# Memory attention: dividing the probabilities before their transposes, and leaving the values product transposed

## Chip, cores, metric
One core of a Trainium2 chip. The metric is the device time of one execution in microseconds (us), the median of three runs. The core has a matrix engine (TensorE, "PE" in the profile; its weight loads are "PEld"), a vector engine (VectorE, "DVE"), an activation engine (ScalarE, "ACT"), a general engine (GpSimd, "POOL") and a queue engine for transfers (SyncE, "SP"). Each works through its own queue in order, and they wait for each other by semaphores.

## The reference, cut to what matters
The kernel is one layer: a state-space mixer beside block attention, then attention over a memory of 256 rows, then a gated convolutional feed-forward network. The change lies in the attention over the memory alone:

```python
def memory_cross_attention(h, mem_n, w_q, w_kv, w_o, qn, kn):
    bsz, t = h.shape[0], h.shape[1]
    m = mem_n.shape[1]
    q = rms_norm((h @ w_q).reshape(bsz, t, X_HEADS, X_HEAD_DIM), qn)
    kv = mem_n @ w_kv
    k = rms_norm(kv[..., :D_X].reshape(bsz, m, X_HEADS, X_HEAD_DIM), kn)
    v = kv[..., D_X:].reshape(bsz, m, X_HEADS, X_HEAD_DIM)
    s = jnp.einsum('bqhd,bmhd->bhqm', q, k).astype(jnp.float32) * (X_HEAD_DIM ** -0.5)
    prob = jax.nn.softmax(s, axis=-1).astype(v.dtype)
    o = jnp.einsum('bhqm,bmhd->bqhd', prob, v).reshape(bsz, t, D_X)
    return o @ w_o
```

There are 512 tokens, 4 heads of width 128, 256 memory rows, and everything is fp32.

## The kernel before
The order of every engine's queue is written out by hand. The 512 tokens are four tiles of 128. The attention over the memory runs in 16 steps, `s = 4 * tile + head`. In step `s` TensorE makes the scores of step `s + 2` (`x_scores`, 128x256 into PSUM), then a "piece" of six 128x512 products with weights (`xq_piece`: the q projection of tiles 2 and 3, up to step 6; `xo_piece`: the output projection, from step 7 on), then the two transposes of the probabilities of step `s` (`prob_transposes`), then the values product of step `s - 1` (`x_values`). In steps 1, 5 and 9 it first transposes the normalised q of the next tile (`qx_transposes`), and in steps 5, 9 and 13 it transposes at the end the attention's output of tile 0, 1 and 2 (`xo_transposes`); that of tile 3 comes among the output pieces after the loop. Products with weights are made of three fp32r products, of high and low halves.

Around it, for every step: VectorE takes the row maximum (`row_max`, line 1855), ScalarE scales it and makes the exponential with its row sum (`x_probabilities`, line 1022) into `pbuf`, which has two slots; the transposed probabilities are copied out of PSUM by ScalarE for even and by VectorE for odd steps (`xp_evac`, line 412 on VectorE). VectorE also evacuates the transposed q (`transposed`, line 1423), and, four steps at a time, divides the output rows by the row sums (`normalise`, lines 1686 and 1420). The transposed output is split into a high half by ScalarE (`xo_hi`) and a low half by VectorE (`xo_lo`, line 1426); both are the left operand of the output projection. The output weights are split into halves too: the high half by ScalarE (`split_hi`, line 498, in steps 5 to 8), the low half by GpSimd (`output_low`, line 976). VectorE adds each finished output tile to the residual (`w_residual`, line 1426).

PSUM has eight banks. `use(bank, name)` in `plan` gives each result its bank in the order of filling; a product that fills a bank waits until the result before it in that bank has been read:

```python
        def fill(pe, name, r=0):

            bank, n = uses[name]
            if n > 0:
                pe.wait_ge(bank_free[bank], r + n)
            return pb[bank]
```

Results are named `xs` (scores), `xp` (transposed probabilities), `xpv` (values product of a tile), `xo` (its transposes), `qxt` (transposed q) and `w00` to `w31` (tile and column half of the output projection). After the 16 steps come the rest of the output projection, the transposes of its normalised rows (`x3_transposes`), and the up projection of the feed-forward network, which is over half of the kernel.

Of the kernel before, what the change touches and what calls it, by code (L numbers as in the profile page):

```python
# [20 lines left out]
TT = T // 128  # L21
# [6 lines left out]
M = 256  # L28
MT = M // 128
XH, XD = 4, 128  # L30
# [75 lines left out]
def layer(nc, A, out):  # L106
# [11 lines left out]
    with ctx:  # L118
# [151 lines left out]
        yasq_ready, yasum_ready = sem("yasq_ready"), sem("yasum_ready")  # L270
        qr_ready = sem("qr_ready")
        conv_ready, gate_ready = sem("conv_ready"), sem("gate_ready")
# [3 lines left out]

        QXT_BANK, XO_BANK, W_BANK = (0, 1, 2, 0), (1, 0, 1, 7), (2, 1, 2, 0, 2, 1, 3, 2)

# [7 lines left out]
        def plan():  # L286
# [38 lines left out]
            for t in range(TT):  # L325
                use(t % 3, f"qx{t}"); use(QXT_BANK[t], f"qxt{t}")

            for s in range(TT * XH):
                use(3 + s % 3, f"xs{s}"); use(6, f"xp{s}")
            for t in range(TT):  # L330
                use(7, f"xpv{t}"); use(XO_BANK[t], f"xo{t}")
                for half in range(2):
                    use(W_BANK[2 * t + half], f"w{t}{half}")
# [679 lines left out]
        def _(act):  # L1013
# [302 lines left out]
            def xo_hi(t):  # L1316
                tile_hi(f"xo{t}", bs[:, 0, :].rearrange("p (a n) -> p a n", a=4)[:, :, t * 128:(t + 1) * 128])

# [17 lines left out]
            for s in range(TT * XH):  # L1336
                if s % 2 == 1:
                    xp_evac(act, lambda o, i: A_(o, i, ACT.Copy), s - 1)
                if s + 1 < TT * XH:
                    x_probabilities(s + 1)  # L1340
                if s in (3, 7):
                    qx_rows(2 + s // 4)
                if s in (6, 10, 14):
                    xo_hi((s - 6) // 4)
                if s in XO_AT:
                    split_hi(act, U_XO + XO_AT.index(s))
                if s == 13:
                    h_square("x3", "w", "x30", 0, 0)
# [60 lines left out]
        def _(dve):  # L1409
# [272 lines left out]

            def normalise(bank, l0, heads, width, t):

                p = read(dve, bank)
                link(V.reciprocal(rl[:, 0:heads], lsum[:, l0:l0 + heads]))
                drained(tt(yrow[:, t, :].rearrange("p (h n) -> p h n", h=heads),
                           p[:, :].rearrange("p (h n) -> p h n", h=heads),
                           rl[:, 0:heads].unsqueeze(2).to_broadcast([128, heads, width]), ALU.mult), bank)
                after_drain(dve, bank)  # L1690

            def tile_lo(name, hi, lo, last=True):
# [133 lines left out]
            def xo_lo(t):  # L1826
                v = [bs[:, i, :].rearrange("p (a n) -> p a n", a=4)[:, :, t * 128:(t + 1) * 128] for i in range(2)]
                tile_lo(f"xo{t}", v[0], v[1])

# [22 lines left out]
            def row_max(s):  # L1852
# [3 lines left out]
                    .then_inc(logit_ready, 1)  # L1856

            row_max(0)
            for s in range(TT * XH):
                if s + 1 < TT * XH:  # L1860
                    row_max(s + 1)
                if s in (5, 9, 13):
                    t = (s - 5) // 4
                    normalise(f"xpv{t}", 32 + XH * t, XH, XD, t)
                if s >= 2 and s % 2 == 0:
# [5 lines left out]
                if s in (2, 6, 10):  # L1871
                    root(f"qx{1 + s // 4}", qr_ready)
                if s in (6, 10, 14):
                    xo_lo((s - 6) // 4)
                if s in (10, 12):
                    w_residual(0, [s // 2 - 5])
                if s == 14:
                    w_residual(1, [0])
                    x3_mean(0)
            xp_evac(dve, V.tensor_copy, TT * XH - 1)  # L1880
            normalise(f"xpv{TT - 1}", 32 + XH * (TT - 1), XH, XD, TT - 1)
            x3_rows(0)
            w_residual(1, [1])
            xo_lo(TT - 1)
            w_residual(2, [0])
# [112 lines left out]
        def _(pe):  # L1998
# [277 lines left out]
            def prob_transposes(pre, sc, s, tiles, ring, last_of_fill=True):  # L2276
                after_drain(pe, f"{sc}{s}")
                p = fill(pe, f"{pre}{s}")
# [29 lines left out]
            def x_values(s):  # L2308
# [3 lines left out]
                for a in range(MT):  # L2312
                    last = mm(p[:, h * XD:(h + 1) * XD], ptb[:, s % 2, a * 128:(a + 1) * 128],
                              xv[:, a, h * XD:(h + 1) * XD], a == 0, a == MT - 1)
                if h == XH - 1:
# [152 lines left out]

            def xo_transposes(t):
                after_drain(pe, f"xpv{t}")  # L2470
                tile_transposes(f"xo{t}", yrow[:, t, :])

            def x3_transposes(t):
# [12 lines left out]
            for s in range(TT * XH):  # L2486
# [8 lines left out]
                else:  # L2495
                    if (s + 1) % XH == 0:
                        after_drain(pe, f"xo{(s + 1) // XH - 2}")
                    xo_piece((s + 1) // XH - 2, (s + 1) % XH)
                prob_transposes("xp", "xs", s, MT, 2)
                if s >= 1:  # L2500
                    x_values(s - 1)
                if s in (5, 9, 13):
                    xo_transposes((s - 5) // 4)
            x_values(TT * XH - 1)
            for i in range(1, 4):
                xo_piece(2, i)
                if i == 2:
                    xo_transposes(3)
            x3_transposes(0)
            after_drain(pe, "xo3")  # L2510
            for i in range(4):
# [84 lines left out]
```

## Time and profile before
| | |
|---|---|
| median of 3 runs | 676.1 us (676.05 to 676.61) |
| profiled execution, its own time | 676.84 us |
| its span in the trace | 675.0 us |
| TensorE busy | 664.4 us (98%) |
| VectorE busy | 489.7 us (73%) |
| ScalarE busy | 345.0 us (51%) |
| GpSimd busy | 178.6 us (26%) |
| granted TensorE clock | full speed, mean 1.00 |
| share of TensorE in the chain that ended last | 82% |

The time of an execution is its span and a little around it. Busy time counts an engine's own work; idle time of an engine that is not the bound costs nothing. In a timeline each row is a start, a length (of all its instructions, where it ends in x2 or more), the engine, the kernel's line, the operation, what it writes and reads, and, where the engine stood idle before it, how long and for whom. Names of tiles are the program's: `pb` is a PSUM bank, `F` a region of a large scratch buffer (q, k, v, rows and transposed probabilities all lie there), `bs` holds the attention's output in halves, `wring` the weights in halves.

### The profile page before, as it was taken

To read this page: it belongs to the slowest core of one execution; us is meant where nothing else is said; L and a number is where in the kernel's file an instruction comes from. 1 tells how busy PE (TensorE), PEld (TensorE's weight loads), DVE (VectorE), ACT (ScalarE), POOL (GpSimd) and SP (SyncE) were. 2 spreads that over 40 slices of the span, in tenths; PEclk is the share of its full clock that TensorE was granted. 3 is DMA by queue.
4 is the path that set the end of the run, shared out by engine and by line. 5 is a ranking of instruction groups with operands and counts; after the bars stand their busy time and mean duration, and the time that the engine had idled before them with its cause. 6 is when DMAs were issued, how large, how long until landed. Compare 5 with 4: busy or idle time off the path is not lost.

```text
span 675.0 us, 10889 instructions
## 1 busy us (share of the span) xinstructions
PE 664.4 (98%) x4039; PEld 550.3 (82%) x4039; DVE 489.7 (73%) x807; ACT 345.0 (51%) x602; POOL 178.6 (26%) x184
## 2 busy tenths in 40 slices
PE   7999999999999999999999999999999999999997
PEld 6978877877778788888998888888888888888886
DVE  3999998849765657556877675666566687867967
ACT  4747654676844544664454433333333454554662
POOL 4899997033221101240101111011101121100000
PEclk9999999999999999999999999999999999999999
DMA  8737563577210215030337557555556446654563
GB/s 257 225 82 183 118 186 102 156 223 258 64 63 2 98 59 187 1 124 1 126 125 249 191 186 242 191 183 187 190 191 227 146 183 210 226 186 141 178 197 124
DMA packets 73919, 105.76 MB, mean 157 GB/s; under 512 B 21929, under 2 KB 48852, under 8 KB 72340
## 3 DMA queue, kind: packets, MB, share of 16 engines
q1 hardware_dynamic: 70612, 98.89, 45.3%
q10 hardware_dynamic: 3264, 6.31, 2.9%
q8 instruction: 25, 0.41, 0.2%
q14 instruction: 18, 0.15, 0.1%
HBM read 88.27 MB, written 17.31 MB: 156 GB/s over the span
## 4 chain that ended last, share of the span: by engine, by line
PE 82%; DMA 4%; POOL 4%; ACT 4%; SPq 3%; DVE 2%; issue 1%; DVEq 0%; ACTq 0%; POOLq 0%
PE pb L519 24%; PE pb L521 24%; PE pb L520 23%; PE pb L2000 7%; PE pb L2003 4%; POOL F L802 2%; ACT F L1022 2%; SPq L679 2%; DMA raw<-in_w_in 1%; DMA F<-F 1%; DMA raw<-in_x_wkv 1%; DVE F L1420 1%; DMA F<-scr_y 1%; SPq L692 0%; ACT xs L1022 0%
## 5 line engine op out<-in xcount | busy, mean ns | idle before, releaser
L519 PE MATMUL pb<-xs,wring 128*128 128x512 f32 (+1 forms) x448 | 165.3, 369 | 0.1
L521 PE MATMUL pb<-xs,wring 128*128 128x512 f32 (+1 forms) x448 | 164.2, 366 | 0.0
L520 PE MATMUL pb<-xs,wring 128*128 128x512 f32 (+1 forms) x448 | 164.1, 366 | 0.0
L1426 DVE SCALAR_TENSOR_TENSOR F<-pb,ccol,F 128x511 f32<-128x511 f32 x88 | 65.9, 749 | 71.7 <-ACT F L1022 69.9
L509 DVE TENSOR_TENSOR wring<-raw,wring 128x1024 fp32r<-128x1024 f32 x73 | 97.5, 1338 | 6.1 <-ACT wring L498 5.9
L519 PE MATMUL pb<-wring,xs 128*128 128x512 f32 x240 | 99.1, 413 | 0.5 <-DVE wring L512 0.3
L519 PEld LDWEIGHTS pb<-xs,wring 128*128 128x128 f32 x448 | 84.5, 189 | 14.5 <-issue 0.6
L521 PEld LDWEIGHTS pb<-xs,wring 128*128 128x128 f32 x448 | 84.5, 189 | 13.7
L520 PEld LDWEIGHTS pb<-xs,wring 128*128 128x128 f32 x448 | 84.5, 189 | 13.5
L521 PE MATMUL pb<-wring,xs 128*128 128x512 f32 x240 | 94.0, 392 | 0.0
L520 PE MATMUL pb<-wring,xs 128*128 128x512 f32 x240 | 93.7, 390 | 0.0
L1022 ACT ACTIVATE F<-pb,ccol 128x512 f32<-128x512 f32 x44 | 34.3, 779 | 115.3 <-PE pb L521 115.1
L498 ACT ACTIVATE wring<-raw 128x1024 fp32r<-128x1024 f32 x78 | 81.8, 1054 | 15.1 <-DMA raw<-in_w_in 6.5
L519 PE MATMUL pb<-wring,bs 128*128 128x512 f32 x170 | 68.6, 404 | 0.6 <-DVE wring L1420 0.5
L828 POOL TENSOR_TENSOR F<-F 128x256 f32<-128x256 f32 x27 | 21.8, 809 | 172.8 <-DVE F L1420 171.4
L521 PE MATMUL pb<-wring,bs 128*128 128x512 f32 x170 | 66.3, 390 | 0.0
L520 PE MATMUL pb<-wring,bs 128*128 128x512 f32 x170 | 66.2, 390 | 0.0
L1022 ACT ACTIVATE F<-pb 16x128 f32<-16x128 f32 (+5 forms) x84 | 31.1, 383 | 56.9 <-PE pb L2003 49.0
L2000 PE MATMUL pb<-F 128*64 128x64 f32 (+6 forms) x1056 | 58.5, 256 | 1.5 <-DVE F L1420 0.7
L2000 PEld LDWEIGHTS pb<-F 128*64 128x64 f32 (+4 forms) x1056 | 45.2, 143 | 14.0 <-issue 10.6
L519 PEld LDWEIGHTS pb<-wring,xs 128*128 128x128 f32 x240 | 45.1, 188 | 12.0 <-issue 1.6
L521 PEld LDWEIGHTS pb<-wring,xs 128*128 128x128 f32 x240 | 45.1, 188 | 10.0
(160 smaller groups left out, 989.6 us busy)
## 6 DMA issues: line engine op xcount, KB each, us to landing
raw<-in_ffn_w_up SPq DMA_DIRECT2D x22, 1024.0 KB, 5.2
F<-in_ffn_w_down SPq DMA_DIRECT2D x11, 1024.0 KB, 5.0
scr_w<-F SPq DMA_DIRECT2D x11, 1024.0 KB, 3.9
F<-in_x SPq DMA_DIRECT2D x8, 512.0 KB, 5.9
raw<-in_w_in ACTq DMA_DIRECT2D x4, 1024.0 KB, 6.0
raw<-in_w_out SPq DMA_DIRECT2D x4, 1024.0 KB, 4.9
raw<-scr_w SPq DMA_DIRECT2D x8, 512.0 KB, 3.8
raw<-scr_w SPq DMA_DIRECT2D x15, 256.0 KB, 4.7
```

The source lines that it names most:

```text
L498: ins = nc.scalar.activation(w_unit(u, 0), raw_unit(u), ACT.Copy)
L509: ins = nc.vector.tensor_tensor(w_unit(u, 1), raw_unit(u), w_unit(u, 0).bitcast(f32), ALU.subtract)
L519: nc.tensor.matmul(ps, lh, rh, start=first, stop=False)
L520: nc.tensor.matmul(ps, lh, rl_, start=False, stop=False)
L521: return nc.tensor.matmul(ps, ll, rh, start=False, stop=last)
L679: sync.dma_start(toep[d * CG:(d + 1) * CG, :, (L - 1 - d) * CG:], kt[0:CG, :, 0:(d + 1) * CG]).then_inc(t_in[q], 16)
L802: return nc.gpsimd.tensor_tensor(o, a, b, ALU.mult)
L828: return nc.gpsimd.tensor_tensor(o, a, b, ALU.subtract)
L1022: return nc.scalar.activation(o, i, f, **k)
L1426: return V.scalar_tensor_tensor(out=o, in0=a, scalar=s1, in1=b, op0=o1, op1=o2)
L2000: return nc.tensor.matmul(o, l, r, start=start, stop=stop)
L2003: return nc.tensor.transpose(o, i, ident[0:i.shape[0], 0:i.shape[0]])
```

## The change
The probabilities are divided by their row sum as soon as the exponential is made, in `pbuf`, before they are transposed (`divide_by_sum`, on VectorE); TensorE's transposes wait for that (`xprob_ready`) and no longer for the exponential. The values product exchanges its operands, so that its result is already transposed: `normalise` and `xo_transposes` go, and `xo_hi` and `xo_lo` read `xpv`. They move one step up, to steps 5, 9 and 13. The banks of `qxt`, `xpv` and `w` are dealt anew.

```diff
-        QXT_BANK, XO_BANK, W_BANK = (0, 1, 2, 0), (1, 0, 1, 7), (2, 1, 2, 0, 2, 1, 3, 2)
+        QXT_BANK, XPV_BANK, W_BANK = (0, 1, 2, 7), (7, 1, 7, 1), (2, 0, 2, 0, 2, 3, 0, 2)
...
             for t in range(TT):
-                use(7, f"xpv{t}"); use(XO_BANK[t], f"xo{t}")
+                if t == 2:
+                    use(QXT_BANK[3], "qxt3")
+                use(XPV_BANK[t], f"xpv{t}")
...
-                if s in (6, 10, 14):
-                    xo_hi((s - 6) // 4)
+                if s in (5, 9, 13):
+                    xo_hi((s - 5) // 4)
...
+            def divide_by_sum(s):
+
+                after_drain(dve, f"xs{s}")
+                link(V.reciprocal(rl[:, s % 2:s % 2 + 1], lsum[:, 32 + s:33 + s]))
+                V.tensor_scalar_mul(pbuf[:, s % 2, 0:M], pbuf[:, s % 2, 0:M], rl[:, s % 2:s % 2 + 1])\
+                    .then_inc(xprob_ready, 1)
+
             row_max(0)
+            divide_by_sum(0)
             for s in range(TT * XH):
                 if s + 1 < TT * XH:
                     row_max(s + 1)
                 if s in (5, 9, 13):
-                    t = (s - 5) // 4
-                    normalise(f"xpv{t}", 32 + XH * t, XH, XD, t)
+                    xo_lo((s - 5) // 4)
...
-                if s in (6, 10, 14):
-                    xo_lo((s - 6) // 4)
                 if s in (10, 12):
                     w_residual(0, [s // 2 - 5])
+                if s + 1 < TT * XH:
+                    divide_by_sum(s + 1)
                 if s == 14:
                     w_residual(1, [0])
                     x3_mean(0)
             xp_evac(dve, V.tensor_copy, TT * XH - 1)
-            normalise(f"xpv{TT - 1}", 32 + XH * (TT - 1), XH, XD, TT - 1)
             x3_rows(0)
+            xo_lo(TT - 1)
             w_residual(1, [1])
-            xo_lo(TT - 1)
...
             def prob_transposes(pre, sc, s, tiles, ring, last_of_fill=True):
-                after_drain(pe, f"{sc}{s}")
+                if pre == "xp":
+                    pe.wait_ge(xprob_ready, s + 1)
+                else:
+                    after_drain(pe, f"{sc}{s}")
...
-                    last = mm(p[:, h * XD:(h + 1) * XD], ptb[:, s % 2, a * 128:(a + 1) * 128],
-                              xv[:, a, h * XD:(h + 1) * XD], a == 0, a == MT - 1)
+                    last = mm(p[:, h * XD:(h + 1) * XD], xv[:, a, h * XD:(h + 1) * XD],
+                              ptb[:, s % 2, a * 128:(a + 1) * 128], a == 0, a == MT - 1)
...
-                if s in (5, 9, 13):
-                    xo_transposes((s - 5) // 4)
             x_values(TT * XH - 1)
             for i in range(1, 4):
                 xo_piece(2, i)
-                if i == 2:
-                    xo_transposes(3)
             x3_transposes(0)
-            after_drain(pe, "xo3")
+            after_drain(pe, "xpv3")
```

On VectorE, in step 9, before (`normalise` of tile 1, the evacuation of q tile 3, maximum 11, the copy of probabilities 9):

```order
L1686 RECIPROCAL rl<-lsum 128x4 [waits bank_full7]
L1420 TENSOR_TENSOR F<-pb,rl 128x512 [waits dve_step]
L1423 TENSOR_SCALAR F<-pb,gcol 128x4x128 [waits bank_full0,bank_free7]
L1855 TENSOR_REDUCE nmx<-pb 128x1 [waits bank_full5]
L412 COPY F<-pb 128x256 [waits bank_full6,bank_full7]
```

And after, from division 9 and maximum 10 (lines are four or five lower in the file's count):

```order
L1856 RECIPROCAL rl<-lsum 128x1 [waits bank_free3]
L1857 TENSOR_SCALAR pbuf<-pbuf,rl 128x256 [waits dve_step]
L1850 TENSOR_REDUCE nmx<-pb 128x1 [waits bank_full4]
L1430 SCALAR_TENSOR_TENSOR bs<-pb,bs 128x4x128 [waits act_hi,bank_full1]
L1427 TENSOR_SCALAR F<-pb,gcol 128x4x128 [waits bank_full7]
L1856 RECIPROCAL rl<-lsum 128x1 [waits bank_free4]
L1857 TENSOR_SCALAR pbuf<-pbuf,rl 128x256 [waits dve_step]
L1850 TENSOR_REDUCE nmx<-pb 128x1 [waits bank_full5]
L416 COPY F<-pb 128x256 [waits bank_full6,bank_full1]
```

The low half of the output (`bs`), with its wait for ScalarE's high half, stands where the normalisation stood, ahead of the evacuation of q, and each maximum stands behind a division, which waits for an exponential.

On ScalarE, in steps 5 and 6, before (copy 4, exponential 6 in two rows from `nmx`, a weight split, exponential 7, the high half of output tile 0):

```order
L1022 ACTIVATE F<-pb 128x256 [waits bank_full6,pv_done]
L1022 ACTIVATE nmx<-nmx,rs 128x1 [waits logit_ready,bank_full3,bank_full6]
L1022 ACTIVATE pbuf,lsum<-pb,nmx,rs 128x256 [waits act_step]
L498 ACTIVATE wring<-raw 128x1024 [waits unit_used,raw_in1]
L1022 ACTIVATE nmx<-nmx,rs 128x1 [waits logit_ready,bank_full4,bank_full6]
L1022 ACTIVATE pbuf,lsum<-pb,nmx,rs 128x256 [waits act_step]
L1022 ACTIVATE bs<-pb 128x4x128 [waits bank_full1]
```

And after:

```order
L1026 ACTIVATE F<-pb 128x256 [waits bank_full6,pv_done]
L1026 ACTIVATE nmx<-nmx,rs 128x1 [waits logit_ready,bank_full3,bank_full6]
L1026 ACTIVATE pbuf,lsum<-pb,nmx,rs 128x256 [waits act_step]
L1026 ACTIVATE bs<-pb 128x4x128 [waits bank_full7]
L502 ACTIVATE wring<-raw 128x1024 [waits unit_used,raw_in1]
L1026 ACTIVATE nmx<-nmx,rs 128x1 [waits logit_ready,bank_full4,bank_full6]
L1026 ACTIVATE pbuf,lsum<-pb,nmx,rs 128x256 [waits act_step]
```

The high half stands ahead of the weight split and of exponential 7.

On TensorE, from the transposes of probabilities 9 to the next piece, before (values 8, output transposes of tile 1, scores 12):

```order
L2003 MATMUL pb<-ident,pbuf 128x128 [waits bank_free6,bank_free3]
L2003 MATMUL pb<-ident,pbuf 128x128
L2000 MATMUL pb<-F 128x128 [waits bank_free7,bank_free6]
L2000 MATMUL pb<-F 128x128
L2003 MATMUL pb<-ident,F 128x128 [waits bank_free0,bank_free7]
L2003 MATMUL pb<-ident,F 128x128 x3
L2000 MATMUL pb<-F 128x256 [waits bank_free3,bank_free0]
L519 MATMUL pb<-wring,bs 128x512 [waits lo_done]
```

And after:

```order
L2004 MATMUL pb<-ident,pbuf 128x128 [waits bank_free6,xprob_ready]
L2004 MATMUL pb<-ident,pbuf 128x128
L2001 MATMUL pb<-F 128x128 [waits bank_free7,bank_free6]
L2001 MATMUL pb<-F 128x128
L2001 MATMUL pb<-F 128x256 [waits bank_free3,bank_free7]
L523 MATMUL pb<-wring,bs 128x512 [waits lo_done]
```

Values 8 wait for bank 7 in both; before, that is the normalisation of tile 1, now it is the evacuation of q tile 3. The transposes of the output are gone.

## Rows read from the trace of the kernel before
**Rows 1.** The page: the span, and TensorE's busy tenths in 40 slices

```profile
span 675.0 us, 10889 instructions
...
PE   7999999999999999999999999999999999999997
```

**Rows 2.** Timeline of TensorE, steps 5 to 7 (start us, length us, work)

```profile
283.76 0.38 PE L2003 MATMUL pb<-ident,pbuf 128*128 128x128 f32 x2
283.98 0.61 PE L2000 MATMUL pb<-F 128*128 128x128 f32 x4
284.43 0.60 PE L2003 MATMUL pb<-ident,F 128*128 128x128 f32 x4
284.86 0.60 PE L2000 MATMUL pb<-F 128*128 128x256 f32 x2
285.11 0.58 PE L519 MATMUL pb<-wring,xs 128*128 128x512 f32 x1
...
286.69 0.38 PE L2003 MATMUL pb<-ident,pbuf 128*128 128x128 f32 x2
...
289.17 0.38 PE L2003 MATMUL pb<-ident,pbuf 128*128 128x128 f32 x2
```

**Rows 3.** Timeline of TensorE, the last output transposes

```profile
314.35 0.60 PE L2003 MATMUL pb<-ident,F 128*128 128x128 f32 x4
314.70 0.48 PE L519 MATMUL pb<-wring,bs 128*128 128x512 f32 x1
```

**Rows 4.** Timeline of TensorE's weight loads, with idle time ahead

```profile
293.30 0.19 PEld L519 LDWEIGHTS pb<-wring,bs 128*128 128x128 f32 x1 [0.34 <-POOL wring L976]
...
323.62 0.19 PEld L519 LDWEIGHTS pb<-xs,wring 128*128 128x128 f32 x1 [0.38 <-issue]
```

**Rows 5.** Timeline of ScalarE in the attention over the memory

```profile
270.47 0.19 ACT L1022 ACTIVATION_READ_ACCUMULATOR pbuf<-pb,nmx,rs 128x1 f32 x1
...
285.07 0.59 ACT L1022 ACTIVATE bs<-pb 128x512 fp32r<-128x512 f32 x1
...
290.67 0.30 ACT L1022 ACTIVATE nmx<-nmx,rs 128x1 f32<-128x1 f32 x1
...
291.56 1.05 ACT L498 ACTIVATE wring<-raw 128x1024 fp32r<-128x1024 f32 x1
292.51 0.37 ACT L1022 ACTIVATE F<-pb 128x256 f32<-128x256 f32 x1
```

**Rows 6.** Timeline of VectorE, steps 9 and 10

```profile
292.52 0.18 DVE L1686 RECIPROCAL rl<-lsum 128x4 f32<-128x4 f32 x1 [1.32 <-PE pb L2000]
...
293.46 0.75 DVE L1423 TENSOR_SCALAR F<-pb,gcol 128x512 f32<-128x512 f32 x1
294.13 0.41 DVE L1855 TENSOR_REDUCE nmx<-pb 128x1 f32<-128x256 f32 x1
295.28 0.42 DVE L412 COPY F<-pb 128x256 f32<-128x256 f32 x1 [0.74 <-PE pb L2003]
...
297.87 0.68 DVE L1426 SCALAR_TENSOR_TENSOR F<-pb,F 128x512 f32<-128x512 f32 x1
```

**Rows 7.** Timeline of GpSimd, subtractions for the output weights' low halves

```profile
283.66 2.37 POOL L976 TENSOR_TENSOR wring<-raw,wring 128x1024 fp32r<-128x1024 f32 x1 [2.52 <-ACT wring L498]
...
290.87 4.71 POOL L976 TENSOR_TENSOR wring<-raw,wring 128x1024 fp32r<-128x1024 f32 x2 [1.79 <-ACT wring L498]
```

**Rows 8.** Timelines of VectorE and GpSimd where both work on SBUF

```profile
33.44 1.59 DVE L1522 TENSOR_SCALAR F<-F 128x1024 f32<-128x1024 f32 x1
...
284.59 1.46 DVE L1420 TENSOR_TENSOR rt<-rs 128x4 f32<-128x4 f32 x1
286.08 0.16 DVE L1420 TENSOR_TENSOR rt<-rt,ms 128x4 f32<-128x4 f32 x1
...
33.42 2.53 POOL L802 TENSOR_TENSOR F<-pw,F 128x512 f32<-128x512 f32 x2
...
59.61 2.08 POOL L802 TENSOR_TENSOR F<-pw,F 128x512 f32<-128x512 f32 x2
```

More of the change, by code:

```diff
@@ L270, in layer @@
         yasq_ready, yasum_ready = sem("yasq_ready"), sem("yasum_ready")
-        qr_ready = sem("qr_ready")
+        qr_ready, xprob_ready = sem("qr_ready"), sem("xprob_ready")
         conv_ready, gate_ready = sem("conv_ready"), sem("gate_ready")
@@ L325, in plan @@
             for t in range(TT):
-                use(t % 3, f"qx{t}"); use(QXT_BANK[t], f"qxt{t}")
+                use(t % 3, f"qx{t}")
+                if t < TT - 1:
+                    use(QXT_BANK[t], f"qxt{t}")
             for s in range(TT * XH):
@@ L1316, in xo_hi @@
             def xo_hi(t):
-                tile_hi(f"xo{t}", bs[:, 0, :].rearrange("p (a n) -> p a n", a=4)[:, :, t * 128:(t + 1) * 128])
+                tile_hi(f"xpv{t}", bs[:, 0, :].rearrange("p (a n) -> p a n", a=4)[:, :, t * 128:(t + 1) * 128])
             qx_rows(0)
@@ L1681, in _ @@
             dve.wait_ge(bias_in, 16)
[L1683 to L1690, printed above, removed]
             def tile_lo(name, hi, lo, last=True):
@@ L1827, in xo_lo @@
                 v = [bs[:, i, :].rearrange("p (a n) -> p a n", a=4)[:, :, t * 128:(t + 1) * 128] for i in range(2)]
-                tile_lo(f"xo{t}", v[0], v[1])
+                tile_lo(f"xpv{t}", v[0], v[1])
             def w_residual(t, halves=range(2)):
@@ L2467, in x_scores @@
                 filled(mm(p[:, 0:M], qT[:, h, t * 128:(t + 1) * 128], kxT[:, h, :]), f"xs{s}")
-            def xo_transposes(t):
-                after_drain(pe, f"xpv{t}")
-                tile_transposes(f"xo{t}", yrow[:, t, :])
             def x3_transposes(t):
@@ L2496, in _ @@
                     if (s + 1) % XH == 0:
-                        after_drain(pe, f"xo{(s + 1) // XH - 2}")
+                        after_drain(pe, f"xpv{(s + 1) // XH - 2}")
                     xo_piece((s + 1) // XH - 2, (s + 1) % XH)
```

## The prediction

> **What bounds the kernel now.** I read the page's head first: of the 40 slices of the 675.0 us span, every one but the first and last shows a 9 for TensorE [rows 1]. So the end moves only where the TensorE queue gets shorter or where it is made to wait. Then I read TensorE's timeline over the attention over the memory, 268 to 323 us, to see how dense it is. One of the 16 steps, from one pair of probability transposes to the next, takes 2.48 us (286.69 to 289.17); a step that also holds four output transposes takes 2.93 us (283.76 to 286.69), and those four own the 0.43 us between 284.43 and 284.86 [rows 2]. The rest of a step is two probability transposes (0.22 us), the values product (0.44 or 0.45), a scores product (0.25) and a weight piece (1.58) [rows 2]. The weight-load timeline, which carries the idle times, shows few waits: 0.34 us at 293.30 for the low half of an output weight, which GpSimd makes, and 0.38 us at 323.62, before the first product of the up projection [rows 4]. So this stage is TensorE bound with thin cover: its helpers are mostly just in time. Last I read those helpers, ScalarE, VectorE and GpSimd, as queues, since the question is what is late once they carry other work.
>
> **What is removed.** Sixteen output transposes. Those of tiles 0 to 2 are worth 0.44 us each; the last four start at 314.35 and the next product at 314.70, 0.35 us, and the piece behind them is no longer interrupted, about 0.1 us more (a restarted piece begins at a larger spacing) [rows 2, 3]. Sum: 3 x 0.44 + 0.45 = 1.77 us of TensorE. The values products keep their shape and number; I cost the exchange of operands at nothing. VectorE loses four normalisations of 0.94 us (292.52 to 293.46) [rows 6], all hidden behind products.
>
> **What is added.** Sixteen times on VectorE a reciprocal of one column (0.16 us, from 0.18 us for four columns [rows 6]), 0.03 us to its wait, and a multiplication of 128x256 from SBUF to SBUF by a per-row scalar. No row shows that form at that size. Above: the copy of 128x256 out of PSUM, 0.42 us [rows 6]. Below: the fixed cost, about 0.16 us. Nearest row: a scalar operation of 128x1024 SBUF to SBUF started at 33.44 and took 1.59 us. GpSimd had started two operations at 33.42 that took 2.53 us together; two like them at 59.61 took 2.08 us, 1.04 each [rows 8]. If the scalar operation was held until the first of the two was done (34.46), it ran 0.57 us for 1024 columns, and held the second in turn (2.08 + 0.57 = 2.65 against 2.53). A quarter of the columns is then about 0.22 us, which I take. The Trainium skill (VectorE: DVE Perf Modes, Mode 2×_2P) says that fp32 scalar operations between SBUF and SBUF use both read ports and go two elements a cycle; its table gives an estimate of (58 + 128) / 0.96 GHz = 0.19 us, with which the sum would be about 0.2 us lower.
>
> **The hold.** A second row shows the same thing inside this very stage: the 128x4 operation at 284.59 takes 1.46 us, where the next one takes 0.16, and ends at 286.05, as the GpSimd subtraction of 283.66 + 2.37 us ends (286.03) [rows 7, 8]. A maximum read from PSUM at 294.13 (0.41 us) goes on undisturbed beside the GpSimd pair of 290.87 to 295.58 [rows 6, 7]. GpSimd makes four such subtractions of 2.37 us here, while divisions 6 to 9 run. I take it that the multiplication is held to the end of the subtraction in flight. The Trainium skill (SBUF — State Buffer, Who interferes with whom) states it as a lock on a port pair that VectorE and GpSimd share, held for a whole instruction; by that rule the trace agrees, and it is a rule against this change.
>
> **The lag of TensorE behind its times of before, step by step.** I carried the three queues forward with the rows' durations: 0.9 us an exponential with the scaling of its maximum, 0.95 a weight split (both by the spacing of 290.67, 291.56 and 292.51), 0.59 a high half [rows 5]; 0.41 a maximum, 0.42 a copy, 0.75 a q transpose's evacuation, 0.68 a residual add, and as much a low half, the same operation on the same shape [rows 6]; 0.05 to 0.1 us from engine to engine.
> - Step 0: the sum is read until 270.66 [rows 5], the division is done near 271.2, and TensorE's transposes (270.9) wait: +0.33.
> - Step 5: no transposes, -0.44. But the low half of output tile 0 now stands ahead of q tile 2's evacuation on VectorE and waits for ScalarE's high half, which stands behind exponential 6: scores 8 wait +0.29.
> - Step 6: division 6 is ready near 285.2, GpSimd is at work from 284.7 to 287.1. Behind it on VectorE stand maximum 7 and the copy of probabilities 5, whose bank TensorE needs: +1.10.
> - Step 8: exponential 7 waited for maximum 7, the second weight split stands behind it on ScalarE, and its low half is done near 292.1: +0.73. At step 9 the wait for a low half is as long as in [rows 4]: 0.
> - Values 8: they now fill bank 7, which q tile 3 leaves only after division 9 (held about 1.3 us), maximum 10, exponential 10, the high half, the low half and the evacuation, near 299.0; TensorE is there at 297.3. +1.75, less the four transposes: -0.44.
> - Step 12: w11 takes bank 0 from w01 (it had bank 0 after bank 1). The add of w01 stands behind a copy that waits for probability transposes 11: 0.38 + 0.05 + 0.34 + 0.68 + 0.07 = 1.52 us from their start (their length, the hand-over, the copy's spacing, the add, the hand-over), where TensorE needs 0.22 + 0.44 + 0.25 = 0.91: +0.61 [rows 2, 6].
> - Step 13: -0.44. Step 15: the add of w10 now stands behind division 15: +0.49.
> - Tail: -0.45, and about -0.1 of small waits that no longer come up.
>
> Waits +5.30, removed -1.77, small -0.1: **+3.4 us**. Beyond 324 us TensorE shows no free time [rows 1], so the lag reaches the end whole. The profiled execution took 676.84 us, 0.74 over the median of 676.1; 676.84 + 3.4 = 680.2, as a median 679.5 us.
>
> **Rivals.** I call a change under 0.2% (1.35 us) no change, about what timing this kernel can tell.
> - *No hold* (the multiplication runs beside GpSimd). For it: reciprocals at 292.52 are not held [rows 6]; against: the two held rows. The terms of steps 6 and 8 go, step 5 shrinks to 0.11, values 8 to 0.61: 0.33 + 0.11 + 0.61 + 0.61 + 0.49 = 2.15, less 1.77 and 0.1 to 0.2: +0.2 us, 676.3. With the multiplication at 0.42 us it is +1.0, 677.1. Not slower. Of this kind is the Trainium skill's rule on the same page that an operation with one SBUF input outside the two-port modes doesn't contend.
> - *Held, and 0.42 us each*: all later terms grow by their share of sixteen times 0.2 us, +5.1 us, 681.2. The row at 33.44 speaks against it.
> - *Faster*: the bank waits of values 8 and step 12 don't arise, because VectorE, with its normalisations gone, reaches the evacuation of q tile 3 and the add of w01 in time. Then only +0.33 stands against 1.77: -1.4 us or a little more, 674.6. It decides at 0.6 us: exponential 10 would have to end that much earlier, and ScalarE's queue from 288 to 294 has hardly a gap [rows 5]. The step 12 term also rests on durations alone.
> - *Partly held*: the multiplications fall between GpSimd's operations more often than I worked out; +1.4 to +3. The mechanism is mine, and it lies in its range.
>
> **Chances.** Forecast with its partial form 0.64, held and slow 0.08, no hold 0.2 (nearly all within 0.2%), faster 0.08. Slower by over 0.2%: 0.72; within: 0.20; faster: 0.08. The range for 8 in 10 runs from the lower no-hold case, 676.3, to the held and slow case, 681.2; the likeliest case's own range is 677.5 to 681.2.
>
> **What would show it.** Right: multiplications on pbuf of about 0.2 us, with some of 1 to 2 us that end with a GpSimd subtraction between 284 and 300; a wait of TensorE of over 1 us before values 8; waits before pieces of tile 1 and 2 of 0.5 us; no output transposes; the first weights of the up projection some 3.4 us after 323.62. Wrong: all multiplications alike in length; values 8 without a wait; the up projection starting within 1 us of before. The forecast falls most easily with the alignment: each hold is the rest of a 2.37 us operation and shifts with whatever shifts before it.

## The result, and the profile after

The changed kernel takes 686.39 us (median of 4 runs, 685.84 to 688.28), the kernel before 676.08 us beside it (4 runs, 675.49 to 676.61): 1.0156 of it, 95% interval 1.0142 to 1.017. It is slower, as forecast, but by 10.3 us and not by 3.4, and outside the range. The profiled execution took 685.96 us, with a span of 684.2 us. Two of the four executions have a mean granted clock of 0.998 (685.84 and 685.96 us), the other two 0.992 and 0.993 (688.28 and 686.83 us); only the one of 685.96 us has a trace.

The page of the kernel after, against [rows 1]:

```profile
span 684.2 us, 10873 instructions
...
PE   8999999999999999979899999999999999999997
```

Between the first and the last slice two stand out that were a 9 before: a 7 (slice 18 of 40, each 17.1 us: 291 to 308 us) and an 8 (slice 20, 325 to 342 us). To say what is lost there, I compare starts of TensorE's work. The work ahead of the stage is the same in every kernel here, and still ends up to 2.2 us earlier or later from one execution to the next (267.38 us in e1, 269.57 in e4), more than half of it made in the first 33 us. So each trace is counted from one common point just ahead of the stage, GpSimd's power for the scales of q tile 0 (the row at 269.31 before, at 269.07 after). Timeline of GpSimd before:

```profile
269.31 1.01 POOL L879 TENSOR_TENSOR rs<-ms,mhalf 128x4 f32<-128x4 f32 x1 [4.40 <-DVE ms L1423]
```

Timeline of TensorE before, the transposes of the probabilities of steps 8, 9, 10 and 12, and the first product of the up projection:

```profile
291.66 0.38 PE L2003 MATMUL pb<-ident,pbuf 128*128 128x128 f32 x2
...
294.79 0.38 PE L2003 MATMUL pb<-ident,pbuf 128*128 128x128 f32 x2
...
297.71 0.38 PE L2003 MATMUL pb<-ident,pbuf 128*128 128x128 f32 x2
...
302.69 0.38 PE L2003 MATMUL pb<-ident,pbuf 128*128 128x128 f32 x2
...
323.65 0.36 PE L519 MATMUL pb<-xs,wring 128*128 128x256 f32 x1
```

Timeline of TensorE after. The rows are the transposes of steps 6, 8 and 9, the first values product of tile 2 ("values 8"), the transposes of steps 10 and 12, the first product of w11, the first product of w20 and the first product of the up projection; the bracket is idle time of the products themselves:

```profile
287.90 0.41 PE L2004 MATMUL pb<-ident,pbuf 128*128 128x128 f32 x2 [0.83 <-DVE F L416]
...
293.48 0.38 PE L2004 MATMUL pb<-ident,pbuf 128*128 128x128 f32 x2
...
297.70 0.44 PE L2004 MATMUL pb<-ident,pbuf 128*128 128x128 f32 x2 [0.82 <-DVE pbuf L1857]
...
301.17 1.32 PE L2001 MATMUL pb<-F 128*128 128x128 f32 x6 [3.03 <-DVE F L1427]
...
304.84 0.63 PE L2004 MATMUL pb<-ident,pbuf 128*128 128x128 f32 x2
...
310.07 0.38 PE L2004 MATMUL pb<-ident,pbuf 128*128 128x128 f32 x2
...
310.98 0.58 PE L523 MATMUL pb<-wring,bs 128*128 128x512 f32 x1
...
316.31 0.47 PE L523 MATMUL pb<-wring,bs 128*128 128x512 f32 x1 [0.88 <-DVE F L1430]
...
332.76 0.35 PE L523 MATMUL pb<-xs,wring 128*128 128x256 f32 x1 [1.93 <-DVE F L1430]
```

Timeline of GpSimd after, the common point and the four subtractions for the output weights' low halves:

```profile
269.07 1.01 POOL L883 TENSOR_TENSOR rs<-ms,mhalf 128x4 f32<-128x4 f32 x1 [4.40 <-DVE ms L1427]
...
284.57 2.38 POOL L980 TENSOR_TENSOR wring<-raw,wring 128x1024 fp32r<-128x1024 f32 x1 [2.64 <-ACT wring L502]
...
289.55 2.38 POOL L980 TENSOR_TENSOR wring<-raw,wring 128x1024 fp32r<-128x1024 f32 x1 [2.61 <-ACT wring L502]
...
292.80 4.70 POOL L980 TENSOR_TENSOR wring<-raw,wring 128x1024 fp32r<-128x1024 f32 x2 [0.86 <-ACT wring L502]
```

Timeline of VectorE after. The rows are divisions 6, 7 and 8, the mean of squares of q tile 3, division 9, the add of w01, and at the end a weight split and the two adds of tile 3:

```profile
285.04 2.06 DVE L1857 TENSOR_SCALAR pbuf<-pbuf,rl 128x256 f32<-128x256 f32 x1
...
288.75 0.35 DVE L1857 TENSOR_SCALAR pbuf<-pbuf,rl 128x256 f32<-128x256 f32 x1
...
290.85 1.23 DVE L1857 TENSOR_SCALAR pbuf<-pbuf,rl 128x256 f32<-128x256 f32 x1
...
293.37 1.82 DVE L1427 TENSOR_SCALAR ms<-sq 128x4 f32<-128x4 f32 x1
...
295.29 2.36 DVE L1857 TENSOR_SCALAR pbuf<-pbuf,rl 128x256 f32<-128x256 f32 x1
...
308.41 0.68 DVE L1430 SCALAR_TENSOR_TENSOR F<-pb,F 128x512 f32<-128x512 f32 x1
...
330.79 1.23 DVE L513 TENSOR_TENSOR wring<-raw,wring 128x1024 fp32r<-128x1024 f32 x1 [0.80 <-ACT wring L502]
...
331.93 1.28 DVE L1430 SCALAR_TENSOR_TENSOR F<-pb,F 128x512 f32<-128x512 f32 x2
```

The lag of TensorE behind its times of before, from these rows (after less before, plus the 0.24 us between 269.31 and 269.07), beside what the prediction's sum had reached at the same place:

| start of | before | after | lag | predicted |
|---|---|---|---|---|
| transposes 6 | 286.69 | 287.90 | 1.45 | 1.28 |
| transposes 8 | 291.66 | 293.48 | 2.06 | 2.01 |
| transposes 9 | 294.79 | 297.70 | 3.15 | 2.01 |
| transposes 10 | 297.71 | 304.84 | 7.37 | 3.32 |
| transposes 12 | 302.69 | 310.07 | 7.62 | 3.93 |
| up projection | 323.65 | 332.76 | 9.35 | 3.43 |

Three places stand out. Up to step 8 the sum holds within 0.2 us. From 8 to 10 it lacks 4 us. Behind step 12, where the sum goes down by 0.5 us, the trace adds 1.7. From the up projection to the end both kernels take the same (684.2 - 332.76 = 351.44 and 675.0 - 323.65 = 351.35 us), so the lag reaches the end whole.

**Steps 8 to 10.** The three rows on pbuf that are longer than 0.35 us, divisions 6, 8 and 9, are held: each ends just behind a GpSimd subtraction (285.04 + 2.06 = 287.10 against 284.57 + 2.38 = 286.95; 290.85 + 1.23 = 292.08 against 289.55 + 2.38 = 291.93; 295.29 + 2.36 = 297.65 against 292.80 + 4.70 = 297.50). The sum named the holds of divisions 6 and 9. It lacked that of division 8, behind which no wait of TensorE stands at transposes 8, and it lacked an operation that I had not thought of as one that can be held: the mean of squares for q tile 3, 128x4, at 293.37, takes 1.82 us instead of 0.17 and ends at 295.19, as the first of the GpSimd pair does (292.80 + 4.70 / 2 = 295.15). The division of step 9 stands behind it and is held by the second of the pair. Nearly the whole 4.70 us of the pair are lost to VectorE's queue. So the transposes of step 9 wait (0.82 us), and values 8, which need the bank that q tile 3 leaves, wait 3.03 us instead of 1.75.

**The clock.** Stretches of the trace after (us of busy time of each engine with the number of its instructions, granted clock of TensorE, share of DMA, GB/s):

```profile
296.00:301.00 5.00, 1.32 (x6) 0.58 (x4) 3.31 (x5) 1.44 (x4) 2.51 (x2) 1.00 0.53 167
302.00:303.00 1.00, 1.00 (x4) 0.82 (x3) 0.90 (x6) 0.87 (x3) 0.00 (x0) 0.50 0.01 2
306.00:307.00 1.00, 1.00 (x6) 0.84 (x5) 0.15 (x1) 0.79 (x3) 0.00 (x0) 1.00 0.00 0
```

From 296 to 301 TensorE was busy for 1.32 us of 5; from 302 to 305 its granted clock is 0.50, the lower of its two levels (1.2 GHz for 2.4). Timeline of TensorE, products at half and at full speed:

```profile
302.71 0.63 PE L524 MATMUL pb<-wring,bs 128*128 128x512 f32 x1
...
303.14 0.63 PE L525 MATMUL pb<-wring,bs 128*128 128x512 f32 x1
...
306.42 0.39 PE L524 MATMUL pb<-wring,bs 128*128 128x512 f32 x1
...
306.65 0.40 PE L525 MATMUL pb<-wring,bs 128*128 128x512 f32 x1
```

They follow each other after 0.43 us in the slow stretch (303.14 - 302.71) and after 0.23 us behind it (306.65 - 306.42). The piece of six took 2.91 us (301.93 to 304.84) instead of 1.58: 1.3 us, and with the four products beside it about 1.5 us. Before, no stretch of this stage was below 1.00.

**The tail.** The first result of the up projection fills bank 0, which after the change is the bank of w30 too. The two residual adds of tile 3 are the last row of VectorE's timeline (331.93, two of them, 1.28 us), behind a weight split at 330.79 that waits for ScalarE; the first is done at about 332.6, and TensorE's product starts at 332.76 after 1.93 us of idle time.

### The profile page after: what moved, and what is told of

Same layout as the page of the kernel before. It is cut to its first block, busy times and chain, and to the rows that moved or that the text cites. A ratio compares the mean times of both kernels' runs of the same rounds, so it can differ in the third digit from the quotient of the medians.

```text
span 684.2 us, 10873 instructions
## 1 busy us (share of the span) xinstructions
PE 666.8 (97%) x4023; PEld 550.7 (80%) x4023; DVE 496.6 (73%) x831; ACT 345.2 (50%) x602; POOL 178.5 (26%) x184
## 4 chain that ended last, share of the span: by engine, by line
PE 79%; DVE 5%; ACT 5%; POOL 4%; DMA 3%; issue 2%; SPq 2%; ACTq 0%; DVEq 0%; POOLq 0%
PE pb L523 23%; PE pb L525 23%; PE pb L524 23%; PE pb L2001 6%; PE pb L2004 4%; POOL F L806 2%; DMA raw<-in_w_in 1%; ACT F L1026 1%; DMA raw<-in_x_wkv 1%; DVE F L1424 1%; SPq L683 1%; DMA F<-scr_y 1%; DVE wring L513 1%; ACT xs L1026 1%; SPq L696 1%
```

## The experiments

The kernels were measured in three groups (e, f, g), each with the kernel before beside it, which stood at 676.0, 676.4 and 676.1 us. A difference across groups carries up to 0.4 us of that. The last column but one of this table counts, in each profiled execution, from the common point to the end of the span, less the 405.69 us (675.0 - 269.31) of before; for the changed kernel it is 684.2 - 269.07 - 405.69 = +9.44. It leaves out the differences of the first 30 us.

| kernel | median us | before beside it | ratio (95%) | stage to end | worked out before the run |
|---|---|---|---|---|---|
| e1 | 679.52 | 675.99 | 1.0057 (1.0036 to 1.0079) | +2.7 | 679.6 |
| e2 | 683.52 | 675.99 | 1.0107 (1.009 to 1.0124) | +7.2 | 684.4 |
| e3 | 680.91 | 675.99 | 1.0074 (1.0055 to 1.0093) | +5.0 | 680 |
| e4 | 681.59 | 675.99 | 1.0084 (1.0063 to 1.0106) | +4.2 | 679.9 |
| f1 | 674.28 | 676.43 | 0.9968 (0.9956 to 0.998) | -1.9 | 674.5 |
| f2 | 673.68 | 676.43 | 0.9966 (0.9952 to 0.998) | -2.1 | 673.9 |
| f3 | 680.48 | 676.43 | 1.0055 (1.0041 to 1.0068) | +3.7 | 681.7 |
| f4 | 675.89 | 676.43 | 0.9993 (0.9983 to 1.0004) | -0.1 | 676.3 |
| g1 | 676.02 | 676.12 | 0.9996 (0.9986 to 1.0007) | -0.1 | 677.7 |
| g2 | 676.79 | 676.12 | 1.0015 (1.0006 to 1.0024) | +1.0 | 676.7 |
| g3 | 675.64 | 676.12 | 0.9996 (0.9987 to 1.0005) | -0.1 | 676.1 |
| g4 | 681.14 | 676.12 | 1.0082 (1.0068 to 1.0096) | +5.1 | 677.5 to 678.5 |

### Parts of the changed kernel taken away

**e1, short GpSimd operations.**
```diff
-nc.gpsimd.tensor_tensor(w_unit(u, 1), raw_unit(u), w_unit(u, 0).bitcast(f32), ALU.subtract)
+nc.gpsimd.tensor_tensor(w_unit(u, 1)[:, :, 0:2], raw_unit(u)[:, :, 0:2],
+                        w_unit(u, 0).bitcast(f32)[:, :, 0:2], ALU.subtract)
```


> The changed kernel, but GpSimd's four subtractions for the output weights' low halves work on 2 of every 512 columns (the rest of those low halves keeps old numbers, so that part of the computation is left out). Theory A (a multiplication or other VectorE operation whose operands all lie in SBUF is held to the end of GpSimd's operation in flight, and all behind it in VectorE's queue with it): every multiplication takes 0.35 us, the waits of TensorE at steps 6, 8 and 9 go, the wait at values 8 falls from 3.2 to about 1.1 us, the clock stays at full speed; time about 3.5 us over before, 679.6 (678.6 to 681). Theory B (the length of VectorE's queue and the round trip from ScalarE make the loss, holds are by the way): at least 8 us over before, 684 or more.

It is 6.9 us faster than the changed kernel (686.39 - 679.52; its four executions lie between 677.57 and 681.19), and by the traces 6.7 (9.44 less 2.7). Every multiplication takes 0.35 or 0.36 us. TensorE's longest wait inside the first 13 steps is now this one, ahead of values 8 (timeline of TensorE):

```profile
294.37 1.12 PE L2001 MATMUL pb<-F 128*128 128x128 f32 x6 [0.88 <-DVE F L1427]
```

0.88 us where the changed kernel has 3.03. The waits of steps 6, 8 and 9 are gone. So GpSimd's long operations own over 6 us of the loss. Not all of it is held work of VectorE: the low halves of the weights come sooner too, and with them go TensorE's waits for those (in the changed kernel's weight loads 0.71 us at 291.98 and 0.44 us at 295.22). In the profiled execution the clock stayed at 1.00, so the difference holds the clock's 1.5 us too.

**e2, w30 in bank 1.**
```diff
-W_BANK = (2, 0, 2, 0, 2, 3, 0, 2)
+W_BANK = (2, 0, 2, 0, 2, 3, 1, 2)
```


> The changed kernel, with the output projection's result w30 in bank 1 and no longer in bank 0. Theory C (the up projection's first product waits 2.3 us because its bank 0 is still held by w30, which VectorE adds late): that wait falls to about 0.4 us, time about 2.0 us under the changed kernel, 684.4. Rival: the wait is for the normalised rows' low halves, as in the kernel before: no change, 686.4.

2.9 us faster than the changed kernel, of which the two traces show 2.3 (9.4 less 7.2, unrounded 2.26); the wait at the up projection is gone (timeline of TensorE, its first product):

```profile
330.39 0.28 PE L523 MATMUL pb<-xs,wring 128*128 128x256 f32 x1
```

The bank of w30 was a term of its own, and my ledger didn't have it.

**e3, no division.** Reciprocals, multiplications and TensorE's wait for them are left out, so the output is not normalised.
```diff
-            divide_by_sum(0)
...
-                if s + 1 < TT * XH:
-                    divide_by_sum(s + 1)
```


> The changed kernel without the division: the reciprocals and multiplications are left out, so the output is not normalised, and TensorE's transposes wait for the exponential. Theory A with the bank waits: no holds of VectorE by 2 us, but the waits for banks stay (values 8 about 0.6, piece of w01 up to 2.3 for the bank of q tile 3, w11 0.6, up projection 2.2): about 4 us over before, 680. Theory B (division is the whole cost): the removed transposes show in full, 1.8 us under before, 674.3.

The time is 680.91, near the 680 expected: half of the loss stays when the division is gone. The nearness is in part luck. The waits for banks at values 8 (0.68 us) and at the up projection (1.92 us) came, but before the first piece of w01, where I had up to 2.3 us for its bank, TensorE waits 2.22 us for a low half of the weights; none came before w11; and there is a hold of 2.38 us, where I had expected none of 2 us. The rows are an operation of VectorE, the GpSimd subtraction beside it, and TensorE's wait:

```profile
286.03 2.38 DVE L1424 TENSOR_TENSOR rs<-rs,rt 128x4 f32<-128x4 f32 x1
...
286.01 2.38 POOL L980 TENSOR_TENSOR wring<-raw,wring 128x1024 fp32r<-128x1024 f32 x1 [0.44 <-ACT wring L502]
...
294.43 0.50 PE L523 MATMUL pb<-wring,bs 128*128 128x512 f32 x1 [2.22 <-POOL wring L980]
```

A 128x4 product of the scale of q tile 2 is held for 2.38 us, the whole of the GpSimd subtraction that started at 286.01. The row maxima behind it are late, hence exponential 8 and ScalarE's weight splits behind it, and TensorE waits 2.22 us for a low half of the output weights. Later TensorE stood for 1.92 us at the up projection, and its clock fell, which the changed kernel's did not at the same wait:

```profile
324.00:326.00 2.00, 0.10 (x1) 0.13 (x2) 2.00 (x3) 0.84 (x1) 0.00 (x0) 1.00 0.00 0
328.00:330.00 2.00, 2.00 (x11) 2.00 (x11) 2.00 (x4) 0.49 (x1) 0.41 (x1) 0.50 0.90 308
```

The columns are those of the stretches above. From the up projection (325.90) to the end this kernel takes 353.20 us against 351.4: 1.8 us for the clock alone, so that 680.91 contains a loss that the expectation didn't.

**e4, exponentials in PSUM.** The multiplication reads PSUM and writes SBUF.
```diff
-drained(A_(pbuf[:, s % 2, 0:M], p[:, 0:M], ACT.Exp, ...), f"xs{s}")
+A_(p[:, 0:M], p[:, 0:M], ACT.Exp, ...).then_inc(xprob_ready, 1)
...
-V.tensor_scalar_mul(pbuf[:, s % 2, 0:M], pbuf[:, s % 2, 0:M], rl[...]).then_inc(xprob_ready, 1)
+drained(V.tensor_scalar_mul(pbuf[:, s % 2, 0:M], p[:, 0:M], rl[...]), f"xs{s}")
```
The division now waits for `xprob_ready`, and TensorE's transposes wait, as in the kernel before, for the scores' bank to be drained, which the multiplication does.


> The changed kernel with the exponential written back to its PSUM bank and the multiplication from there to SBUF; the whole computation stands. Theory A: a read of PSUM is not held, each multiplication about 0.42 us whatever GpSimd does; time about 3.8 us over before, 679.9 (678.9 to 681.5), and no fall of the clock. Theory B: the same number of operations, each a little longer, so no faster than the changed kernel, 686 or more.

All 16 multiplications take 0.48 us (0.483 to 0.485), beside GpSimd's subtractions or not, where those on SBUF take 0.35 and up to 2.36. The time, 681.59, is 0.1 us above the range I gave: the direction holds, and the size is 1.7 us worse than worked out. From the common point on, though, the profiled execution loses 4.2 us where 3.9 were worked out, so most of the 1.7 us isn't made in the stage. Ahead of it the granted clock was 0.50 from 13 to 16 us, and all four executions have a mean granted clock of 0.997, where the kernel before beside them has 0.999 or 1.000. What the stage still loses is mostly waits for banks and for a low half of the weights, 0.98 us at 295.26, 0.94 at 297.83 (values 8), 1.28 at 311.64 and 2.32 at 328.06 in the weight loads.

### The order mended, and undone piece by piece

**f1, all orders mended.** e4 and e2 together, with:
```diff
-XO_AT = [5, 6, 7, 8]
+XO_AT = [4, 6, 7, 8]
...
             row_max(0)
+            row_max(1)
...
-                if s + 1 < TT * XH:
-                    row_max(s + 1)
+                if s + 2 < TT * XH:
+                    row_max(s + 2)
...
-                if s in (5, 9, 13):
-                    xo_lo((s - 5) // 4)
+                if s in (6, 10, 14):
+                    xo_lo((s - 6) // 4)
...
-                if s in (10, 12):
-                    w_residual(0, [s // 2 - 5])
+                if s in (9, 11):
+                    w_residual(0, [(s - 9) // 2])
```
The high halves (`xo_hi`) move like `xo_lo`, and the add of w10 from step 14 to 13.

> The changed kernel with exponentials written in place in PSUM and the multiplication bringing them to SBUF (0.48 us each, never held), row maxima taken two steps ahead instead of one, high and low halves of the output tiles back in steps 6, 10, 14, the first weight split one step earlier, the first three residual adds at steps 9, 11, 13 instead of 10, 12, 14, and output tile 3's first half in bank 1 instead of 0. The whole computation is kept. Theory A (all of the 10.3 us beyond the transposes is waits made by the order of the queues, the banks and the holds): the queues carried forward by hand give -1.5 us against before, so 674.5 us (673.9 to 676.2), waits of TensorE left: 0.6 at step 0, 0.3 at the last values product. Theory B (a cost that no order takes away, such as the exchanged operands, or the sixteen removed transposes being worth nothing): 676.5 or more.

674.28, and 0.9968 of before. It beats both kernels. These are all its waits of weight loads in the stage that exceed 0.1 us:

```profile
270.12 0.20 PEld L2006 LDWEIGHTS pb<-ident,pbuf 128*128 128x128 f32 x2 [0.81 <-DVE pbuf L1858]
...
308.61 0.52 PEld L2003 LDWEIGHTS pb<-F 128*128 128x128 f32 x4 [0.33 <-DVE F L416]
```

Theory B is gone: the exchanged operands cost nothing that could be seen.

**f2, no division in the mended kernel.** f1 without reciprocals and multiplications and with exponentials to SBUF; the output is not normalised.

> As the mended kernel, but with no reciprocals and no multiplications at all (the probabilities stay undivided, so the output is not normalised), exponentials into SBUF as before. It measures what removing the output transposes and normalisations is worth when nothing is added. Theory A: -2.1 us against before, 673.9 us (673.2 to 674.9), TensorE waits for nothing over 0.3 us in the stage. Theory B (the exchanged operands eat the gain): 676. The ledger of the prediction had -1.77 and -0.1 of small waits, so 674.1.

-2.1 us by the traces, -2.75 by the medians: the sixteen transposes and the small waits are worth at least what the prediction gave them (1.77 + 0.1). The division, once its place is right, costs 0.2 to 0.6 us (f1 against f2).

**f3, the division alone.** The kernel before with `divide_by_sum` in its places and, for the normalisation, a copy:
```diff
-drained(tt(yrow[:, t, :]..., p[:, :]..., rl[:, 0:heads]..., ALU.mult), bank)
+drained(V.tensor_copy(yrow[:, t, :], p[:, :]), bank)
```


> The kernel before with the division alone: reciprocal and multiplication of each step added in their places on VectorE, the normalisation turned into a plain copy (0.4 us in place of 0.9), output transposes, banks and all other orders as before. The whole computation is kept. Theory A (the division with its holds is itself the larger part, whatever the order): +5.7 us against before, 681.7 us (680 to 684), with waits of TensorE at step 0 of 0.5, at a low half near 292 to 294 of 1 us, and before pieces of the first two output tiles of 0.5 each. Theory C (the division is harmless without the new banks and the earlier low halves): 676 to 677.5.

+4.05 us by the medians. VectorE's timeline shows division 7 held, and that of the weight loads the wait for a low half:

```profile
288.26 1.87 DVE L1859 TENSOR_SCALAR pbuf<-pbuf,rl 128x256 f32<-128x256 f32 x1
...
296.14 0.19 PEld L519 LDWEIGHTS pb<-wring,bs 128*128 128x128 f32 x1 [1.86 <-POOL wring L976]
```

Theory C is gone; the division needs no new banks to do harm.

**f4, mended but held.** f1 with the multiplication from SBUF to SBUF.

> The mended kernel with the multiplication from SBUF to SBUF as the change has it, so that GpSimd can hold it. The whole computation is kept. Against the mended kernel it shows what the holds alone still cost when the order has slack: by the queues carried forward +1.8 us, so 676.3 us (675.5 to 678), with held multiplications of over 1 us at two or three steps and waits of TensorE at steps 7 and 9 and before values 8 of 0.4 to 0.8. If a hold costs nothing once the maxima are ahead (theory D), it is as fast as the mended kernel, 674.5.

1.6 us slower than f1. Timeline of VectorE:

```profile
286.38 2.01 DVE L1857 TENSOR_SCALAR pbuf<-pbuf,rl 128x256 f32<-128x256 f32 x1
...
291.84 2.37 DVE L1857 TENSOR_SCALAR pbuf<-pbuf,rl 128x256 f32<-128x256 f32 x1
```

The holds are as long as in the changed kernel, but with the maxima ahead and the banks free they cost 1.6 us, and not the 6.9 that e1 took away. Theory D is gone too. At 0.9993 (0.9983 to 1.0004) f4 is no faster than the kernel before: the gain of f1 needs the exponentials in PSUM as well as the order.

**g1, g2, g3: one thing undone in f1** (the adds' steps; the halves' steps; the maxima ahead).

> The mended kernel (f1) with one thing undone: the three residual adds of the first output tiles back at steps 10, 12, 14. The whole computation is kept. Theory A, order (w11 now takes the bank of w01 and so needs w01's add early): the queues carried forward by hand give +3.4 us against the mended kernel, 677.7 us (676.3 to 678.5), with waits of TensorE of 0.6, 1.8 and 1.0 before the first pieces of w10, w11 and w20. Rival: the adds' place is harmless, since TensorE has slack there; 674.3.

> The mended kernel with one thing undone: high and low halves of the output tiles at steps 5, 9, 13, where the change put them. The whole computation is kept. Theory A: +2.4 us against the mended kernel, 676.7 us (675.5 to 677.5), with waits of TensorE of 0.6 before probability transposes 7, 0.7 and 0.5 before output weight pieces and 0.6 before values 8. Rival: the low half may stand there without cost; 674.3.

> The mended kernel with one thing undone: each row maximum one step ahead, where both kernels have it. The whole computation is kept. Theory A: +1.85 us against the mended kernel, 676.1 us (675 to 677), most of it late exponentials, hence late weight splits on ScalarE and a wait for a low half of 0.5 us. Rival: the maxima have slack enough; 674.3.

Against f1 they cost 1.7, 2.5 and 1.4 us by the medians as they stand, where 3.4, 2.4 and 1.85 were worked out. Taken each against the kernel before of its own group it is 2.0, 2.8 and 1.7 us, and by the traces 1.8, 2.9 and 1.8. In g1 the waits before w10 and w20 came (0.70 and 1.29 us), the one of 1.8 us before w11 didn't, and that is what was worked out too much. In g2 a low half of the weights is late, as the timeline of weight loads shows:

```profile
293.97 0.19 PEld L523 LDWEIGHTS pb<-wring,bs 128*128 128x128 f32 x1 [1.27 <-POOL wring L980]
```

g3 has 0.57 us at the same place, and 0.93 ahead of a piece at 307.73. Each of the three alone takes most or all of the gain of f1 away; only g2 is measurably slower than before.

**g4, the division alone from PSUM.** f3 with the edit of e4.

> The kernel before with the division alone, as in the division-alone kernel, but with the exponentials in place in PSUM, and the multiplication PSUM to SBUF (0.48 us, never held). The whole computation is kept. Theory A (the holds are most of what the division alone costs): by the queues carried forward +2.2 us against before; as those gave 5.7 for the held form where 4.0 was measured, 677.5 to 678.5 us. Rival (the length of the VectorE queue costs it, not the holds): as the division alone, 680 or more, since the multiplication is 0.13 us longer.

A miss: 681.14, no better than f3 and 3 us over what I expected. The trace says why. The rows are GpSimd's subtractions, VectorE's 128x4 operations on the scale of q tile 2, and the weight load that waits:

```profile
283.48 2.38 POOL L976 TENSOR_TENSOR wring<-raw,wring 128x1024 fp32r<-128x1024 f32 x1 [2.12 <-ACT wring L498]
...
286.23 2.34 POOL L976 TENSOR_TENSOR wring<-raw,wring 128x1024 fp32r<-128x1024 f32 x1 [0.36 <-ACT wring L498]
...
284.11 1.77 DVE L1420 TENSOR_TENSOR rt<-rs 128x4 f32<-128x4 f32 x1
...
286.32 2.27 DVE L1420 TENSOR_TENSOR rs<-rs,rt 128x4 f32<-128x4 f32 x1
...
289.24 0.19 PEld L519 LDWEIGHTS pb<-wring,bs 128*128 128x128 f32 x1 [2.18 <-DVE bs L1426]
```

The multiplications are free of holds, so VectorE reaches the scale of q tile 2 while the subtractions run, and two of its four small operations are held for 1.77 and 2.27 us, each to the end of a subtraction (285.88 against 285.86; 288.59 against 288.57). The low half of output tile 0 stands behind them, and TensorE waits 2.18 us for it. I had called the multiplications the holds; VectorE's small operations on SBUF are of the same kind. But held operations are not all of it. At the up projection TensorE is 5.04 us behind its times of before: 2.07 arise at this wait, 0.96 at a wait for a low half of the weights (1.27 us at 295.81), 0.92 by transposes 2 (275.36, with the common point at 267.90), and 1.04 in step 15 (1.34 us at 312.17), where the add of w10 stands behind division 15. In the last two places GpSimd has no subtraction under way, so about 2 us are what the division adds to VectorE's queue without any hold, as the rival has it.

## Why the prediction was right, and where it was wrong

- **What is removed**: right. 1.77 and 0.1 us predicted, 2.1 to 2.75 measured (f2); exchanged operands at nothing: right.
- **Division, size**: 0.22 us taken, 0.35 measured. The 0.57 us that I worked out for 1024 columns from the rows at 33.44 and 59.61, scaled down to 256, gave too little. Of itself it is small: step 0 has 0.41 us of lag instead of 0.33 (271.06 against 270.89, plus 0.24). At transposes 2 the lag is 0.65 (276.26 against 275.85, plus 0.24); the sum has nothing for this rise.
- **The hold**: right as a mechanism, and the main one. e1 shows it. The Trainium skill (SBUF — State Buffer, Who interferes with whom) says that VectorE's two-port operations, and those with two SBUF inputs while GpSimd reads SBUF, lock GpSimd out or are locked out for a whole instruction; by that rule the traces agree, down to 128x4 operations of 2.38 us.
- **Steps 5, 6 and 8**: right within 0.2 us each, in part by luck: the lag at transposes 6 (1.45 us for 1.28) holds the 0.24 us from transposes 0 to 2 that the sum lacks, while steps 5 and 6 gave 0.78 us where it has 0.95.
- **Step 9 "0", and values 8 "+1.75"**: this is the step of the prediction that failed. I carried one hold (division 9, about 1.3 us) into values 8. Measured: 1.82 us for the mean of squares and 2.36 for division 9, back to back, hence 1.1 us more lag at step 9 and 3.03 us of idle time at values 8, and then about 1.5 us of half clock. Lag from step 8 to step 10: 5.31 us, where the sum had 1.31. I had shown a held 128x4 operation in [rows 8], and then looked for holds on multiplications alone.
- **Step 12 (+0.61)**: didn't come, and none stands before w11 in g1 either, where TensorE isn't late. The durations of the term were right: the add of w01 ends 1.51 us after the start of transposes 11 (308.41 + 0.68 against 307.58), where it has 1.52. Its place was wrong. In the order of the queue the piece behind transposes 11 is still one of w10; w11 begins a step later, behind transposes 12, at 310.98, 1.9 us after the add is done.
- **Step 15 (+0.49)**: right in kind, 0.88 us.
- **Tail (-0.45 and -0.1, "the lag reaches the end whole")**: the second step that failed. I followed the new banks to w11 and not to w30; 1.93 us of idle time, taken away by e2 for 2.3 to 2.9 us.
- **Rivals**: "no hold" is refuted by e1 and e4. "Held, and 0.42 us each" came nearer in size, but spread evenly what lies in a few long waits.

The misses add up to the 5.9 us between predicted (3.43) and measured lag (9.35): 1.1 at step 9, 2.9 at values 8 with the clock, -0.4 at step 12, 2.2 behind it. The other 0.95 us between this lag and the medians' 10.3 are made up thus: the profiled execution of before was 0.76 us over the median beside it, that of the changed kernel 0.43 us under its own, and 0.24 us go off for the common point. How often the clock falls after a wait stays open, and so does why it fell in e3 at the up projection and not in the changed kernel, e1 and e4 at an equal wait. Where it fell longer in the two slowest executions of the changed kernel no trace shows.

## What to carry to other kernels

When an engine that others lean on gets an operation that can be held, look for every operation of its queue that lies under the other engine's long one, small ones too: they are held one after the other, and the one freed of the hold uncovers the next (g4). Follow each changed bank or buffer to the next stage that takes it. A change that costs 10 us by waits can still gain 2 us when each new step gets a place in which its result is early and the operation that could be held reads PSUM (f1; f4 has the places alone and gains nothing that could be measured): judge the order, not the operation.

## What the runs showed of the hardware that was not expected

- Operations of 128x4 on VectorE that take 0.16 us alone took 1.77, 1.82, 2.27 and 2.38 us beside a GpSimd subtraction of 2.38 us (g4, the changed kernel, g4, e3). Reciprocals of one column (0.15 to 0.16 us) and maxima and copies out of PSUM (0.41 us) went on undisturbed.
- The multiplication of 128x256 by a per-row value takes 0.35 us from SBUF to SBUF and 0.48 us from PSUM to SBUF. Of these only the first is held in any trace here: those from PSUM take 0.48 or 0.49 us in e4, f1 and g1 to g4.
- TensorE's granted clock fell to 0.50 about a microsecond after it had begun to work again behind a wait of 3.03 us, stayed there from 302 to 305 and was back at 1.00 from 306; in e2 the same came behind a wait of 3.02 us (0.50 from 302 to 304). Behind a wait of 1.92 us in e3 it fell too; behind waits of 1.93, 1.93 and 1.92 us at the same place in the changed kernel, e1 and e4 it didn't.
